# Solving the DeltaNet chunks: inverting the triangle's first five levels on compact blocks of 32, in a two-layer hybrid decoder step

## What is computed

```python
def gated_delta_chunked(q, k, v, g, beta, s0):
    ...
    kk = jnp.einsum('nbhid,nbhjd->nbhij', kc, kc)
    m = jnp.where(strict, bc[..., :, None] * kk * decay, 0.0)
    a_mat = m + jnp.eye(CHUNK, dtype=m.dtype)
    rhs = jnp.concatenate([vc * bc[..., None], kc * (bc * jnp.exp(G))[..., None]], axis=-1)
    sol = lax.linalg.triangular_solve(a_mat, rhs, left_side=True, lower=True, unit_diagonal=True)
    ...

def gated_delta_recurrent(q, k, v, g, beta, s0):
    def step(s, xs):
        q_t, k_t, v_t, g_t, b_t = xs
        s = s * jnp.exp(g_t)[..., None, None]
        u = b_t[..., None] * (v_t - jnp.einsum('bhk,bhkv->bhv', k_t, s))
        s = s + jnp.einsum('bhk,bhv->bhkv', k_t, u)
        return s, jnp.einsum('bhk,bhkv->bhv', q_t, s)
```

## Time and profile before

| | us |
|---|---|
| median of 3 runs (lowest, highest) | 1544.36 (1543.38, 1550.44) |
| the profiled execution | 1544.28 |
| its span in the trace | 1542.5 |
| TensorE busy in it | 1511.4 (98%) |
| start of level 1 on TensorE to the first instruction behind level 6 | 223.40 to 284.61 |

### The profile page before, as it was taken

The page is one execution under the profiler, slowest core; times in us unless marked ns, Lnnn a source line. Parts: engine busy times, 40 slices in busy tenths (PEclk is TensorE's granted clock), DMA queues, the critical chain, the costliest instruction groups (busy, mean ns, idle before and its releaser), DMA issues.

```text
span 1542.5 us, 32756 instructions
## 1 busy us (share of the span) xinstructions
PE 1511.4 (98%) x14439; PEld 1013.8 (66%) x14439; DVE 561.0 (36%) x944; ACT 354.5 (23%) x583; POOL 59.5 (4%) x100
## 2 busy tenths in 40 slices
PE   8999999899999999999999999999999999999997
PEld 8989888899999999845354454454453566533332
DVE  6767878666665577411101101101101101111113
ACT  6566544444444453300000000000000000000001
POOL 0000031000000000020000000000000000000010
PEclk9999999999999999999999999999999999999999
DMA  6764358254554575699999999999999999999994
GB/s 265 294 243 165 110 191 263 82 194 167 190 181 162 182 301 197 273 398 418 419 399 420 419 402 419 412 408 420 403 418 420 401 419 419 402 419 419 418 416 186
DMA packets 78051, 491.02 MB, mean 318 GB/s; under 512 B 9304, under 2 KB 9560, under 8 KB 53216
## 3 DMA queue, kind: packets, MB, share of 16 engines
q1 hardware_dynamic: 70000, 460.77, 75.0%
q0 software_dynamic: 7920, 28.25, 5.6%
HBM read 465.07 MB, written 23.92 MB: 317 GB/s over the span
## 4 chain that ended last, share of the span: by engine, by line
PE 79%; DMA 6%; DVE 6%; SPq 4%; ACT 3%; issue 1%; DVEq 0%; ACTq 0%
PE PP L2308 33%; PE PP L1738 22%; PE PP L2318 15%; DMA ring<-in_w_down 2%; SPq L453 2%; DVE dlo L369 2%; SPq L457 2%; DMA ring<-in_w_up 2%; ACT dhi L363 2%; PE PP L2051 1%; PE PP L2061 1%; DMA ring<-in_mkv 1%; PE PP L1856 1%; PE PP L1840 0%; PE PP L2191 0%
## 5 line engine op out<-in xcount | busy, mean ns | idle before, releaser
L2308 PE MATMUL PP<-ring,gen 128*32 128x448 f32 x6144 | 582.8, 539 | 2.7 <-DVE gen L1592 1.2
L2308 PEld LDWEIGHTS PP<-ring,gen 128*32 128x32 f32 x6144 | 294.6, 110 | 287.1 <-issue 259.9
L2318 PE MATMUL PP<-ring,gen 128*32 128x512 f32 x2688 | 293.2, 592 | 1.8 <-DMA ring<-in_w_down 1.8
L2318 PEld LDWEIGHTS PP<-ring,gen 128*32 128x32 f32 x2688 | 112.2, 110 | 179.0 <-issue 159.9
L1738 PE MATMUL PP<-uh,dhi 128*128 128x264 f32 x736 | 213.9, 291 | 3.3 <-DVE dlo L369 2.4
L1676 DVE TENSOR_TENSOR gen<-ubuf,PP 128x448 f32<-128x448 f32 x48 | 27.0, 617 | 519.7 <-PE PP L2308 519.7
L369 DVE TENSOR_TENSOR dlo<-ring,dhi 128x2048 fp32r<-128x2048 f32 (+2 forms) x85 | 175.5, 2065 | 96.8 <-ACT dhi L363 96.5
L1738 PE MATMUL PP<-ul,dhi 128*128 128x264 f32 x736 | 209.6, 285 | 0.0
L1738 PE MATMUL PP<-uh,dlo 128*128 128x264 f32 x736 | 209.3, 284 | 0.0
L938 ACT ACTIVATE ubuf<-PP 128x448 f32<-128x448 f32 x48 | 22.6, 544 | 783.2 <-PE PP L2308 783.2
L363 ACT ACTIVATE dhi<-ring 128x2048 fp32r<-128x2048 f32 (+2 forms) x85 | 147.1, 1731 | 108.4 <-PE PP L1738 80.4
(11 more groups left out here) (453 smaller groups left out, 1362.4 us busy)
## 6 DMA issues: line engine op xcount, KB each, us to landing
ring<-in_w_up SPq DMA_DIRECT2D x256, 896.0 KB, 25.3
ring<-in_w_down SPq DMA_DIRECT2D x112, 1024.0 KB, 25.6
ring<-in_wi SPq DMA_DIRECT2D x22, 1024.0 KB, 4.8
ring<-in_a_in SPq DMA_DIRECT2D x18, 1024.0 KB, 4.8
ring<-in_wo SPq DMA_DIRECT2D x16, 704.0 KB, 4.1
slot_rows<-ring POOLq DMA_DIRECT2D x25, 384.0 KB, 15.7
ring<-in_mkv SPq DMA_DIRECT2D x8, 1024.0 KB, 5.1
ring<-in_kc SPq DMA_DIRECT2D x8, 1024.0 KB, 9.7
```

Of the source, the lines that this page charges most:

```text
L2308: mm = pe.matmul(bank((c // KD % 2) * SG + g)[SL * q:SL * (q + 1), 0:FQ], xs[:, at_:at_ + SL], w[:, q * FQ:(q + 1) * FQ], start=(k == 0), ...
L2318: return pe.matmul(out[SL * quarter:SL * (quarter + 1), :], hT[:, at_:at_ + SL], w[:, k * D + h * 512:k * D + (h + 1) * 512], start=(j == ...
```

## The change

**Compact blocks.** The diagonal blocks of 32 x 32 (4 in each matrix, 8 heads) are kept as tiles of 128 x 256, block b on partitions 32b to 32b+31, head x in columns 32x to 32x+31. T32 is the transpose of the inverse so far, U32 the inverse itself, V32 and W32 hold products; all four lie in the space of Tb. Levels 1 to 4 run on them, and level 5 starts from them. A level is now, for each chunk: `blocks`: 8 products with 32-column weights, heads x and x+4 in the same 32 columns of the array, four such tiles side by side, into one half bank; a copy by ScalarE (V32); `turned`: 2 transposes of 128 x 128; a copy by ScalarE (W32); `blocks` again, against the whole Ub; `block_step` by VectorE (a product with a mask, out of PSUM, 128 x 256); `turned`; `new_blocks` by VectorE: a subtraction from T32, then a 32 x 32 transpose into U32. The second `blocks` reads the inverse as full 128 x 128 matrices, so U32 is spread into the diagonal of Ub at each level: bands 0 and 1 by ScalarE, bands 2 and 3 by GpSimd (`whole_blocks`, two copies each of 32 x 256 a chunk). MLb holds the diagonal blocks of M for all of these levels, so `level_mask` goes away; three masks of 128 x 1024 remain (`masked`: level 5 for both chunks, and level 6 for both).

**Level 5** runs in the same form with ScalarE in place of `block_step`; VectorE then transposes out of PSUM and copies the two new blocks of each matrix into Ub (`pair_blocks`). **Level 6** is what it was: full products.

**The state.** GpSimd multiplies the state by its fade, 64 instructions of 128 x 128 (`faded_state`, 16 between the spread blocks of successive levels, the first 16 after `sd_mm`), and VectorE's `new_state` is only an addition, 4 instructions of 128 x 512 a level in place of 16.

**Queues.** The 25 zeroing stores are started once `ain_mm` has reached 31, in place of after the state has landed, and ahead of the store of the convolution's output. The four stores of the new state go from GpSimd's queue to SyncE's, behind the loads of the state. GpSimd sets both Ub to zero.

The diff, cut to its core:

```diff
@@ new_state
+            for g in gs:
+                v.wait_ge(s("state_faded"), 4 * r + g + 1)
                 v.wait_ge(s("sd_outer"), 4 * r + g + 1)
-                for q in range(4):
-                    n = 16 * r + 4 * q + g
-                    sl = state[:, n * P:(n + 1) * P]
-                    ins_ = v.scalar_tensor_tensor(out=sl, in0=sl, scalar=sgb[:, n:n + 1], in1=bank(4 + g)[:, q * P:(q + 1) * P],
-                                                  op0=ALU.mult, op1=ALU.add)
-                ins_.then_inc(s("state_new"), 1)
+                sl = state[:, 16 * r * P:16 * (r + 1) * P].rearrange("p (q g c) -> p q g c", q=4, g=4)[:, :, g, :]
+                v.tensor_tensor(sl, sl, bank(4 + g).rearrange("p (q c) -> p q c", q=4), ALU.add).then_inc(s("state_new"), 1)
@@ SyncE, behind the loads of the state
+                    for x in range(4):
+                        sp.wait_ge(s("state_new"), 4 * (x + 1))
+                        sp.dma_start(outs["state"][x], state[:, x * DCH:(x + 1) * DCH]).then_inc(s(f"state_stored{x // 2}"), 16)
@@ GpSimd
-            pool.wait_ge(s("conv_state"), 2)
-            store(outs["conv"], convio)
             pool.wait_ge(s("ones_set"), 6)
-            pool.wait_ge(s("state_loaded"), 64)
+            pool.wait_ge(s("ain_mm"), 31)
             for i in range(NST + 1):
                 pool.dma_start(step_rows[i].rearrange("p (j n) -> p j n", j=4), zrow[0:C].unsqueeze(1).to_broadcast([C, 4, 256]))\
                     .then_inc(s("rows_zeroed"), 16)
-            for i in range(4):
-                pool.wait_ge(s("state_new"), 4 * (i + 1))
-                pool.dma_start(outs["state"][i], state[:, i * DCH:(i + 1) * DCH]).then_inc(s(f"state_stored{i // 2}"), 16)
+            def whole_blocks(lv, c):
+                pool.wait_ge(s("dl_uf"), 2 * lv + c + 1)
+                for b in (2, 3):
+                    ins_ = pool.tensor_copy(diagonal(c, b), U32[c][32 * b:32 * b + 32].rearrange("p (x j) -> p x j", x=H))
+                ins_.then_inc(s("dl_up"), 1)
+            def faded_state(r):
+                for g in range(4):
+                    for q in range(4):
+                        n = 16 * r + 4 * q + g
+                        ins_ = pool.tensor_scalar(state[:, n * P:(n + 1) * P], state[:, n * P:(n + 1) * P], sgb[:, n:n + 1], None, ALU.mult)
+                    ins_.then_inc(s("state_faded"), 1)
+            whole_blocks(0, 0)
+            pool.wait_ge(s("sd_mm"), 1)
+            faded_state(0)
+            whole_blocks(0, 1)
+            for lv in range(1, NB):
+                for c in range(2):
+                    whole_blocks(lv, c)
+                if lv < 4:
+                    faded_state(lv)
@@ TensorE
+            def blocks(c, out, left, right):
+                for x in range(H):
+                    q, g = x % 4, x // 4
+                    mm = pe.matmul(out[32 * q:32 * q + 32, g * P:(g + 1) * P], left[c][:, 32 * x:32 * x + 32], right[c][:, head(x)],
+                                   start=True, stop=True)
+            def turned(c, out):
+                for g in range(2):
+                    mm = pe.transpose(out[:, HALF + g * P:HALF + (g + 1) * P], V32[c][:, g * P:(g + 1) * P], ident)
+            for lv in range(1, NB + 1):
+                    ...
+                    blocks(c, bank(2 * c), T32, MLb if lv < NB else Xb)
+                    ...
+                    turned(c, bank(2 * c))
+                if 2 <= lv:
+                    outer(lv - 2)
+                    ...
+                    pe.wait_ge(s("dl_ua"), 2 * (lv - 1) + c + 1)
+                    pe.wait_ge(s("dl_up"), 2 * (lv - 1) + c + 1)
+                    blocks(c, bank(2 * c + 1), W32, Ub)
+                    ...
+                    turned(c, bank(2 * c + 1))
```

More of the change, by code:

```diff
@@ L157, in build @@
         iota = consts[:, CIOTA:CIOTA + P]
+        near, step5, step6 = (consts[:, CLVL + i * P:CLVL + (i + 1) * P] for i in range(3))
+        step32 = [consts[:, CMASK + 32 * lv:CMASK + 32 * lv + 32] for lv in range(NB)]
+        unit32 = consts[:, CUNIT:CUNIT + 32]
         h = hbuf[:, :].rearrange("p (k t) -> p k t", k=KD)
@@ L239, in build @@
         ktail = [cut(gen, SC + 3072, 1024), cut(ring, 3072, 1024)]
+        T32, U32, V32, W32 = ([cut(b, HALF * i, HALF) for b in Tb] for i in range(4))
         Sb = cut(gen, SC + 5840, 1024)
@@ L796, in _ @@
                     a.activation(urow, bank(6)[:, 0:P], ACT.Copy).then_inc(s("sd_row"), 1)
+                for c in range(2):
+                    if lv < NB:
+                        whole_blocks(lv, c)
+                    else:
+                        a.wait_ge(s("dl_mm"), products(lv, 2, c))
+                        a.activation(V32[c], bank(2 * c + 1)[:, 0:HALF], ACT.Copy, scale=-1.0).then_inc(s("dl_ev"), 1)
+            for step, dst in ((0, Tb), (1, Xb)):
+                for st in range(4):
+                    a.wait_ge(s("dl_mm"), 8 * NB + 4 * step + st + 1)
+                    a.activation(half(dst[st // 2], st % 2), bank(st), ACT.Copy).then_inc(s("dl_ev"), 1)
             def inverted(c):
@@ L1278, in _ @@
             v.wait_ge(s("dl_mt"), 2)
-            first_level(0)
+            first_blocks(0)
             value_rows(1, PP[3])
@@ L1282, in _ @@
             v.wait_ge(s("dl_mt"), 4)
[L1283 to L1285 removed]
+            first_blocks(1)
             def sample_rows():
@@ new lines, in pair_blocks @@
+            def pair_blocks(c):
+                v.wait_ge(s("dl_mm"), products(NB, 3, c))
+                link(v.transpose(U32[c], bank(2 * c + 1)[:, HALF:2 * HALF]))
+                for b in (0, 2):
+                    ins_ = v.tensor_copy(Ub[c][32 * b:32 * b + 32].rearrange("p (x k) -> p x k", x=H)[:, :, 32 * b + 32:32 * b + 64],
+                                         U32[c][32 * b + 32:32 * b + 64].rearrange("p (x j) -> p x j", x=H))
+                ins_.then_inc(s("dl_um"), 1)
+            for lv in range(1, NB + 1):
@@ L1325, in _ @@
-                if lv + 1 < NLVL:
-                    level_mask(lv + 1, 1)
+                if 2 <= lv:
+                    new_state(v, lv - 2, (0, 1))
+                if lv < NB:
+                    for c in range(2):
+                        block_step(lv, c)
+                    for c in range(2):
+                        new_blocks(lv, c)
+                else:
+                    for c in range(2):
+                        masked(c, MLb, step6, products(NB - 1, 0, c))
+                    for c in range(2):
+                        pair_blocks(c)
@@ L2043, in _ @@
                     pe.transpose(bank(7)[:, 0:P], kqrow, ident).then_inc(s("sd_mm"), 1)
-                if 2 <= lv < 6:
-                    outer(lv - 2)
-                for st in range(4):
-                    c = st // 2
-                    pe.wait_ge(s("dl_ml"), 2 * lv + c + 1)
-                    pe.wait_ge(s("dl_t"), n0 + st + 1)
-                    for x in four(st):
-                        mm = pe.matmul(PP[c][:, head(x)], MLb[c][:, head(x)], Tb[c][:, head(x)], start=True, stop=True)
-                    mm.then_inc(s("dl_xx"), 1)
+                for c in range(2):
+                    pe.wait_ge(s("dl_ev"), copies(lv, 0, c))
+                    turned(c, bank(2 * c))
                 if lv == 1:
```

158 lines of the change are left out of this document (105 added, 53 removed).

## The result

The changed kernel takes 1560.34 us (median of 4 runs, 1559.02 to 1562.01), the kernel before, run beside it, 1546.57 (1543.38 to 1550.44, 4 runs): a ratio of 1.0098, 95% interval 1.0086 to 1.0111. It is 13.8 us slower by these medians and 15 by the ratio; 1535.4 had been predicted, with a range that ended at 1547. The profiled execution took 1560.93 us, with a span 16.8 us longer than before. `solve`, at 284.61 in the kernel before (284.88 on its chain), begins at 300.54, 15.9 us later. So the loss lies in the inversion and passes on to the end, as the prediction had assumed for its gain.

The account below looks back on a forecast made before the run. TensorE was taken to bound the kernel before, and a chain of short steps the changed levels. `solve` moving from 284.6 to 275.7 gave 8.9 us less, 1544.3 - 8.9 = 1535.4 us, range 1529 to 1547.

Parts of the forecast that it names:

- What bounds the kernel: TensorE bounds the levels before the change, 61.2 us; a shift of `solve` at 284.61 passes whole to the end.
- Step 1: VectorE's work ahead of level 1: both chunks ready at 228.3, where level 1 used to start at 223.40.
- Step 2: Early zero stores delay the state to about 226; with the pass over it partly at half speed, level 1 starts at 232.0.
- Step 3: Level 1: GpSimd's first 16 fades, 0.30 us each, precede chunk 1's blocks; level 1 takes 6.9 us, level 2 starts at 238.9.
- Step 4: Levels 2 to 4: a chain of 6.6 us a level, with VectorE's 5.4 and GpSimd's 6.1 us of work fitting; to 258.6.
- Steps 5 and 6: Level 5 reaches the full products at 266.8, 8.2 us later; level 6 takes 8.9 as before, ending at 275.7.
- GpSimd becomes the bound: Rival, levels 2 to 4: fades of 0.45 gain 3.8 us, 0.53 nothing, from 0.63 over 7.7 us slower; chance 14%.
- The slow clock: Rival: TensorE's steps doubled through whole levels by a falling clock, 1547 us; chance 17%.
- The small tiles don't overlap: Rival: small products at 110 ns each, a level's `blocks` 7 us, gain gone, 1545 us; chance 4% with anything else.
- The state was not in time: Rival that the state's loads win over the zeros: level 1 starts at 228.3, 14.4 us less, 1529.9; chance 15%.
- all zeros did not go first: Rival that all zero stores precede the state, which lands at 235: 1544.5 us; chance 5%.

Follow-up runs that it names:

- e18: Changed kernel with zero stores behind the state's loads, all block copies on GpSimd, fades half on ScalarE, half fused on VectorE; 1532.0 us, ratio 0.9919.
- e4: Kernel before with its zero stores started early, at `ain_mm` 31 in place of after the state has landed; 1555.0 us, ratio 1.0071.
- e2: Changed kernel with the zero stores on SyncE's queue, behind the state's loads; 1550.6 us, ratio 1.0041.
- e1: Changed kernel with the fade back in VectorE's fused update, GpSimd only copying blocks; 1545.1 us, ratio 1.0003.
- e13: Changed kernel with GpSimd fading only 64 of the 128 columns of each block; 1548.8 us, ratio 1.0022.
- e3: Changed kernel with fades fused on VectorE and the zero stores behind the state's loads; 1539.5 us, ratio 0.9968.
- e16: e14 with fewer extra products, level 1's eight kept; 1532.6 us, ratio 0.9925.
- e8: e3 with extra, unread products on TensorE where it waits; 1534.5 us, ratio 0.9927.
- e12: Kernel before with GpSimd fading the state, VectorE only adding, state and zero stores on SyncE, zero stores behind the state's loads; 1543.9 us, ratio 1.0002.
- e14: e8 with all block copies on GpSimd and the fades of two of four groups on ScalarE; 1535.0 us, ratio 0.9930.
- e17: e14 with no extra products but level 1's eight; 1531.4 us, ratio 0.9916.
- e5: Changed kernel with ScalarE copying all four bands of blocks and GpSimd doing only the fades; 1555.6 us, ratio 1.0068.
- e9: Changed kernel with the extra TensorE products of e8 in the same places; 1560.3 us, ratio 1.0108.

## Why the prediction was wrong, by its steps

Starts in us: as predicted, in the changed kernel, and in e18, whose placement takes away both the late state and the fades ahead of block copies:

| | predicted | changed | e18 |
|---|---|---|---|
| level 1 | 232.0 | 233.8 | 223.9 (chunk 1: 228.5) |
| level 2 | 238.9 | 247.2 | 234.7 |
| level 3 | 245.5 | 254.3 | 242.0 |
| level 4 | 252.0 | 264.5 | 249.0 |
| level 5 | 258.6 | 276.3 | 255.6 |
| full transposes | 266.8 | 289.7 | 263.6 |
| `solve` | 275.7 | 300.5 | 272.8 |

**What bounds the kernel: right.** A shift of `solve` passed on to the end to within 3 us: 8.9 later in e4 gave 10.0 more, 11.8 earlier in e18 gave 12.5 less by its ratio; e2, 8.6 later, gave 5.6 more, and e1, 2.5 later, no difference.

**Step 1, right by luck in part.** VectorE had both chunks' blocks at 228.4 (228.3 predicted). The sum over 1024 numbers was mis-sized, 1.89 us and not 1.2; the run before it began earlier by as much.

**Step 2, right in its mechanism.** The pass over the state began at 227.4, behind a wait of 10 us; 226 had been forecast from the turns of the two queues, and e4 confirms the cause alone, in the kernel before. TensorE had been idle for 10 us and not 6. The clock was at 0.50 before the pass and until 232.2, nearly all of it and not half, so it took 6.0 us and not 5.4. Level 1 was 1.8 us late. (The terms of this step add up to 231.6; 232.0 was carried on.)

**Step 3, the step that failed.** "I take 0.30" for a fade that takes 0.60, above the 0.53 that was meant as its far end. The bounds came from zeroing rows, which give 0.8 ns a column and a fixed part of 0.1 us, and from VectorE's price; a fade has 2.5 ns a column and a fixed part of 0.29. Level 1 took 13.3 us, not 6.9. The copies of 32x256 took 0.40, not 0.33.

**Step 4, failed by the same term.** "Both just fit" was 6.1 us of GpSimd's work in a level of 6.6. With 11.2 nothing fits: levels 2 to 4 took 7.1, 10.3 and 11.8 us.

The chain's sum of 6.6 was too low as well. In e13's level 3 TensorE waits for no copy of GpSimd, the clock is 1.00 and the layout is the changed kernel's:

```profile
252.66 0.65 PE L2122 MATMUL PP<-ring,gen 128*32 128x128 f32 x16
...
259.79 0.65 PE L2122 MATMUL PP<-ring,gen 128*32 128x128 f32 x16 [0.18 <-DVE gen L1376]
```
```profile
252.18 0.42 DVE L1376 TENSOR_TENSOR gen<-gen,PP 128x256 f32<-128x256 f32 x1
...
257.16 1.28 DVE L394 TENSOR_TENSOR ring<-ring,PP 128x512 f32<-128x512 f32 x2 [1.41 <-PE PP L2113]
258.36 0.42 DVE L1371 TENSOR_TENSOR gen<-PP,consts 128x256 f32<-128x256 f32 x1
```

It takes 7.13 us. From the first subtraction to ScalarE's copies for chunk 1 it is 1.8 us, not 1.15; and `block_step` (258.36) stands on VectorE behind two additions that wait for the outer products, so that it starts 1.36 behind `blocks` (257.00) and not 0.72. The other terms together were counted 0.75 too high and hide a part of that. With the fused updates of e1 and e3 a level took 7.9, with VectorE busy for 7.1 to 7.3 of it. e18's level 4 comes to 6.59, but with no block copies ahead of ScalarE's evictions: its agreement with the forecast's 6.6 is luck. e16 to e18 mend ScalarE's queue and VectorE's load at once, which leaves open how much each is worth alone.

**Steps 5 and 6.** 13.4 us in place of 8.2, with a wait of 5.34 for GpSimd, and 10.8 in place of 8.9, at a clock of 0.50 from 283.4 to 293.6 us.

**The miss as a sum.** 1.8 (level 1's start) + 6.4 (level 1) + 9.4 (levels 2 to 4) + 5.2 (level 5) + 1.9 (level 6) = 24.7 us, against 24.8 between 275.7 and 300.5. By the runs, in time: 15 us are the fades on GpSimd (changed kernel against e1, with VectorE's fused update in their place). The other 10 are e1 against the forecast. In starts e1 is 11.4 behind it: 2.9 at level 1's start, -1.4 in level 1, 5.5 in levels 2 to 4, 1.6 in level 5, 2.8 in level 6. The sum of the chain, the fused updates that e1 itself brings back and the clock, which cost e3 5 us, have a part in that; no run separates them.

**The rivals.** "GpSimd becomes the bound" came true, and had 14%. Its own scale (gain gone at 0.53, 7.7 us slower from 0.63) foretells 8 us slower for the measured mean of 0.635 (40.6 us for 64); 13.8 to 15 were measured, since it built on the forecast's other terms. The slow clock had 17%, and the range's upper end, 1547, is its case: TensorE's steps doubled through whole levels. No run shows that; the clock did fall in the changed kernel, to 0.50 in five stretches of 3.4 to 10.3 us between 221.9 and 293.6, and in e3 all of its falls together cost the 5 us of e8. "The small tiles don't overlap" was wrong: the second chunk's 16 products started 0.46 us behind the first's (233.83 and 234.29), 29 ns each. The state was not in time, and all zeros did not go first: it landed at 227.4, between 218.7 and 235.

**GpSimd beside VectorE.** GpSimd's copies take 0.40 us alone; beside a mask of VectorE (248.99 to 250.40) the two took 2.08, one of them 1.30, and that mask 1.41 in place of 1.22. This set little in the changed kernel, where 64 fades took 40.6 us in place of 64 x 0.60, 2 us more; in e12 it stretched GpSimd's work, to 48.7 us for 64 fades, at no cost, and in e18 it lies behind the wait of 1.46 us in level 2. Fades of 0.60 stand against 0.26 a block for VectorE's fused update, with one more input: more than a factor of two at 128 columns.

## What to carry to other kernels

An engine whose trace shows no computing has no price: before work is moved to it, bound its instruction by a fixed part and a part per column, and take for the far end the point at which the conclusion turns. Here that point, 0.53, lay within a factor of two of the guess, and a chance of 14% was too small for it. What cost most here was a slow bulk task (16 fades, 9.5 to 11.0 us) on one engine's queue ahead of a short one on which the critical chain waits in each round, 3.0 to 7.1 us each time; the same bulk task with nothing behind it, in a kernel that TensorE bounds (e12), cost nothing (ratio 1.0002). And when a chain of short steps replaces a full TensorE, look where each copy stands in its engine's queue: moving the fades, the block copies and the start of the zero stores made 28 us of difference between the changed kernel and e18, with the same products.

## What the runs showed of the hardware

- GpSimd multiplying 128x128 numbers by a scalar per partition: 0.60 us (changed kernel), 128x64: 0.45 (e13). A copy of 32x256: 0.40 (changed kernel). ScalarE does the 128x128 in 0.29 start to start (e14, e17, e18), VectorE fuses it with an addition in 0.26.
- Beside VectorE's masks single fades of GpSimd took as long as 1.54 us (2.38 in e12), beside its `block` (L1366) 0.82 to 0.91, while VectorE's masks took at most 1.41, 0.19 us longer than alone.
- VectorE's sum over 1024 numbers read with a stride took 1.89 us (changed kernel, L1288), where a two-input pass over 1024 in order takes 1.22.
- The granted clock was at 0.50 behind waits of 2.9 us (e5) and 3.9 us (e3, ahead of level 1's second chunk), while behind one of 3.0 us in the changed kernel it fell only at 262.9; with waits of 1.2 and 1.6 us a level it stayed at 1.00 for three levels of e3 and then fell at 258.7 us. Keeping TensorE busy was worth 5 us where TensorE was on the chain (e8 against e3) and nothing where GpSimd was (e9, 1560.3 as the changed kernel).
